# Latent attention: rotary without a permutation matrix, and the softmax of two heads issued in a row

## What is computed

```python
def _rope(x, base):
    ...
    x1, x2 = x[..., :half], x[..., half:]
    return jnp.concatenate([x1 * cos - x2 * sin, x2 * cos + x1 * sin], axis=-1)

def _shared_latent_kv(x, w_down, kv_norm, w_up):
    c = x @ w_down
    lat = _rms_norm(c[..., :KV_LORA], kv_norm)
    k_rope = _rope(c[..., KV_LORA:], ROPE_BASE_B)
    kv = (lat @ w_up).reshape(b, s, H_B, QK_NOPE + V_HEAD)
    return kv[..., :QK_NOPE], k_rope, kv[..., QK_NOPE:]

def block(args):
    sc = (jnp.einsum('bqhd,bkhd->bhqk', qn_i, k_nope)
          + jnp.einsum('bqhr,bkr->bhqk', qr_i, k_rope)).astype(jnp.float32) * scale
    sc = jnp.where(kpos[None, :] <= qpos[:, None], sc, -jnp.inf)
    p = jax.nn.softmax(sc, axis=-1).astype(v.dtype)
    return jnp.einsum('bhqk,bkhd->bqhd', p, v)
```

## Time and profile before

| | before |
|---|---|
| median of 3 runs | 897.47 us (897.4 to 897.61) |
| the profiled execution | 896.96 us |
| its span, first to last instruction | 895.6 us |
| TensorE busy | 887.7 us, 99% of the span |
| VectorE busy | 595.9 us, 67% |
| ScalarE busy | 496.7 us, 55% |
| GpSimd busy | 80.0 us, 9% |
| granted TensorE clock | 1.0 throughout |

### The profile page before, as it was taken

How to read it: one execution, slowest core, us unless ns; L and a number is a source line. 1 busy time by engine, 2 the same in 40 slices (tenths; PEclk the granted TensorE clock), 3 DMA queues, 4 the chain that set the end, 5 groups by cost and what they waited for, 6 DMA issues and landing times.

```text
span 895.6 us, 13337 instructions
## 1 busy us (share of the span) xinstructions
PE 887.7 (99%) x5601; PEld 790.5 (88%) x5601; DVE 595.9 (67%) x801; ACT 496.7 (55%) x629; POOL 80.0 (9%) x58
## 2 busy tenths in 40 slices
PE   9999999999999999999999999999999999999998
PEld 8798887888999999999787899999999888888887
DVE  5876566559866666666568887869767656557441
ACT  6454444435656666666436578797854454545330
POOL 0010101000001111111000000032200011221000
PEclk9999999999999999999999999999999999999999
DMA  9834554642653444455572645423445634545620
GB/s 346 327 131 185 188 194 182 206 154 69 241 184 114 145 147 147 149 188 188 181 257 98 232 147 184 141 95 106 147 172 188 230 127 161 188 166 214 250 98 23
DMA packets 24828, 154.37 MB, mean 172 GB/s; under 512 B 3136, under 2 KB 3520, under 8 KB 9024
## 3 DMA queue, kind: packets, MB, share of 16 engines
q1 hardware_dynamic: 22880, 148.97, 46.1%
q10 hardware_dynamic: 1728, 4.02, 1.6%
q0 software_dynamic: 160, 0.52, 0.1%
HBM read 152.46 MB, written 1.05 MB: 171 GB/s over the span
## 4 chain that ended last, share of the span: by engine, by line
PE 96%; DVE 2%; ACT 1%; DMA 1%; issue 0%; SPq 0%; ACTq 0%
PE ps L338 25%; PE ps L340 25%; PE ps L339 25%; PE ps L389 7%; PE ps L392 3%; PE ps L612 1%; PE ps L637 1%; DMA w_raw<-in_a_w_in 1%; PE ps L617 1%; PE ps L779 1%; PE ps L411 1%; PE ps L807 1%; PE ps L518 1%; PE ps L796 1%; PE ps L627 1%
## 5 line engine op out<-in xcount | busy, mean ns | idle before, releaser
L1420 DVE TENSOR_TENSOR w_lo_ring<-w_raw,w_hi_ring 128x2048 fp32r<-128x2048 f32 x146 | 337.0, 2320 | 183.4 <-ACT w_hi_ring L965 183.2
L965 ACT ACTIVATE w_hi_ring<-w_raw 128x2048 fp32r<-128x2048 f32 x146 | 277.4, 1910 | 109.0 <-PE ps L340 103.7
L338 PE MATMUL ps<-xT_hi,w_hi_ring 128*128 128x256 f32 x520 | 149.4, 287 | 0.5 <-DVE w_lo_ring L1426 0.5
L339 PE MATMUL ps<-xT_lo,w_hi_ring 128*128 128x256 f32 x520 | 147.0, 283 | 0.0
L340 PE MATMUL ps<-xT_hi,w_lo_ring 128*128 128x256 f32 x520 | 147.0, 283 | 0.0
L338 PE MATMUL ps<-w_hi_ring,xT_hi 128*128 128x512 f32 (+1 forms) x272 | 107.4, 395 | 1.4 <-DVE xT_lo L1597 0.6
L340 PE MATMUL ps<-w_hi_ring,xT_lo 128*128 128x512 f32 (+1 forms) x272 | 104.4, 384 | 0.0
L339 PE MATMUL ps<-w_lo_ring,xT_hi 128*128 128x512 f32 (+1 forms) x272 | 104.3, 383 | 0.0
L338 PEld LDWEIGHTS ps<-xT_hi,w_hi_ring 128*128 128x128 f32 x520 | 99.6, 192 | 3.0 <-issue 2.1
L339 PEld LDWEIGHTS ps<-xT_lo,w_hi_ring 128*128 128x128 f32 x520 | 99.6, 192 | 0.6
L340 PEld LDWEIGHTS ps<-xT_hi,w_lo_ring 128*128 128x128 f32 x520 | 99.6, 192 | 0.0
(11 more groups left out here) (328 smaller groups left out, 1647.8 us busy)
## 6 DMA issues: line engine op xcount, KB each, us to landing
w_raw<-in_a_w_in SPq DMA_DIRECT2D x22, 1024.0 KB, 4.9
w_raw<-in_w_ff_in SPq DMA_DIRECT2D x16, 1024.0 KB, 4.9
w_raw<-in_w_ff_out SPq DMA_DIRECT2D x16, 1024.0 KB, 4.8
w_raw<-in_b_w_uq SPq DMA_DIRECT2D x16, 576.0 KB, 4.4
w_raw<-in_a_w_out SPq DMA_DIRECT2D x8, 1024.0 KB, 4.9
w_raw<-in_b_w_gate SPq DMA_DIRECT2D x8, 1024.0 KB, 5.0
w_raw<-in_kv_w_up SPq DMA_DIRECT2D x8, 1024.0 KB, 4.8
w_raw<-in_b_w_out SPq DMA_DIRECT2D x8, 1024.0 KB, 4.8
```

The lines of the kernel that those rows point to most:

```text
L338: k.T.matmul(out, lh, rh, start=start, stop=False, skip_group_check=True)
L339: k.T.matmul(out, lh, rl, start=False, stop=False, skip_group_check=True)
L965: k.A.activation(k.hi[:, u % RING, :], k.raw[u % RING][:, :], ACT.Copy).then_inc(k.s["w_hi"], 1)
L1420: k.V.tensor_tensor(k.lo[:, u % RING, :], k.raw[u % RING][:, :], k.hi[:, u % RING, :].bitcast(F32), ALU.subtract).then_inc(k.s["w_lo"], 1)
```

## The change

The permutation matrix, its table, the copy `b_xr` and the semaphores `b_xr`, `b_rotated`, `b_cos` and `b_sin` go. VectorE multiplies the rotary part by the cosines straight from PSUM, and by the sines in four instructions of 32 partitions each, that write to the partner's 32 partitions (n to n ^ 1); the sign is now in the table of sines. GpSimd only adds. The softmax of a head is in two functions: `dve_masked` and `dve_normal`. VectorE masks both heads in a row, then does `dve_lo(k, u + 1 + AHEAD)`, then normalises both heads; ScalarE exponentiates both heads in a row, ahead of `act_hi(k, u + 1 + AHEAD)`. The output stage has a like order for the last pair. The core of the diff:

```diff
@@ place_latent
-    k.b_rope, k.b_rot, k.b_mask = (k.place(n, s) for n, s in (("ropeB", [P, 2, S]), ("rotB", [P, P]), ("maskB", [P, 3 * P])))
+    k.b_rope, k.b_mask = (k.place(n, s) for n, s in (("ropeB", [P, 2, S]), ("maskB", [P, 3 * P])))
@@ pe_pair
     if pair == 0:
-        T.wait_ge(s["b_xr"], 1)
-        T.matmul(ps[:, 7, 0:S], k.b_rot[:, :], k.b_xr[:, :], start=True, stop=True).then_inc(s["b_rotated"], 1)
         T.wait_ge(s["b_lat"], 1)
...
             if q == 2 and n == 0 and pair:
-                T.wait_ge(s["b_sin"], pair)
+                T.wait_ge(s["b_turned"], pair)
...
-    T.wait_ge(s["b_xr"], pair + 2)
-    T.matmul(ps[:, 2, S:2 * S], k.b_rot[:, :], k.b_xr[:, :], start=True, stop=True).then_inc(s["b_rotated"], 1)
@@ act_pair
     if pair:
         act_exps(k, pair - 1, 0)
+        act_exps(k, pair - 1, 1)
...
     if pair:
         act_pT(k, pair - 1, 0)
-        act_exps(k, pair - 1, 1)
     act_hi(k, u + 3 + AHEAD)
@@ act_attention_output
     act_exps(k, last, 0)
+    act_exps(k, last, 1)
     act_hi(k, U_BOUT + 2 + AHEAD)
     act_pT(k, last, 0)
-    act_exps(k, last, 1)
@@ dve_latents
-    V.tensor_copy(k.b_xr[:, :], ps[:, 6, 0:S]).then_inc(s["b_xr"], 1)
+def dve_rotary(k, x):
+    k.V.tensor_tensor(k.b_xc[:, :], x, k.b_rope[:, 0, :], ALU.mult)
+    for n in range(4):
+        src, dst = slice(32 * n, 32 * n + 32), slice(32 * (n ^ 1), 32 * (n ^ 1) + 32)
+        m = k.V.tensor_tensor(k.b_xs[dst, :], x[src, :], k.b_rope[src, 1, :], ALU.mult)
+    return m
@@ dve_key_rotary
+    own.mark(dve_rotary(k, k.ps[:, 6, 0:S]))
     own.wait()
+    k.V.tensor_tensor(k.b_kr, k.b_xc[:, :], k.b_xs[:, :], ALU.add).then_inc(k.s["b_kr"], 1)
@@ dve_masked: dve_softmax as far as b_pmax; dve_normal: the rest of it
+def dve_normal(k, pair, h):
+    V, s, own, i = k.V, k.s, k.v_own, 2 * pair + h
     V.wait_ge(s["b_pexp"], i + 1)
     own.mark(V.reciprocal(k.b_rsum[:, h, :], k.b_rsum[:, h, :]))
     own.wait()
+    for q, cols in enumerate((slice(0, P), slice(P, 3 * P))):
         m = V.tensor_scalar(k.b_p[:, h, cols], k.b_p[:, h, cols], k.b_rsum[:, h, q:q + 1], None, ALU.mult)
     m.then_inc(s["b_p"], 1)
@@ dve_pair
     if pair:
-        dve_softmax(k, pair - 1, 0)
+        dve_masked(k, pair - 1, 0)
+        dve_masked(k, pair - 1, 1)
...
     dve_lo(k, u + 1 + AHEAD)
+    if pair:
+        dve_normal(k, pair - 1, 0)
+        dve_normal(k, pair - 1, 1)
     dve_lo(k, u + 2 + AHEAD)
     V.wait_ge(s["w_used"], u + 3)
     if pair:
-        V.wait_ge(s["b_cos"], pair)
-    V.tensor_copy(k.b_xr[:, :], ps[:, 2, 0:S]).then_inc(s["b_xr"], 1)
-    if pair:
-        dve_softmax(k, pair - 1, 1)
+        V.wait_ge(s["b_qr"], pair)
+    else:
+        V.wait_ge(s["b_kr"], 1)
+    dve_rotary(k, ps[:, 2, 0:S]).then_inc(s["b_turned"], 1)
     dve_lo(k, u + 3 + AHEAD)
     if pair:
         dve_og(k, pair - 1)
-    V.wait_ge(s["b_rotated"], pair + 2)
-    if pair:
-        V.wait_ge(s["b_qr"], pair)
-    V.tensor_tensor(k.b_xs[:, :], ps[:, 2, S:2 * S], k.b_rope[:, 1, :], ALU.mult).then_inc(s["b_sin"], 1)
@@ dve_attention_output
-    dve_softmax(k, last, 0)
+    dve_masked(k, last, 0)
+    dve_masked(k, last, 1)
+    dve_normal(k, last, 0)
     dve_lo(k, U_BOUT + 2 + AHEAD)
-    dve_softmax(k, last, 1)
+    dve_normal(k, last, 1)
@@ pool_program
-        G.wait_ge(s["b_xr"], pair + 2)
...
-        G.tensor_tensor(k.b_xc[:, :], k.b_xr[:, :], k.b_rope[:, 0, :], ALU.mult).then_inc(s["b_cos"], 1)
-        G.wait_ge(s["b_cos"], pair + 1)
-        G.wait_ge(s["b_sin"], pair + 1)
+        G.wait_ge(s["b_turned"], pair + 1)
         G.tensor_tensor(k.b_qr[:, pair % 2, :], k.b_xc[:, :], k.b_xs[:, :], ALU.add).then_inc(s["b_qr"], 1)
@@ constants
+    sign = np.where(np.arange(P)[:, None] % ROPE < ROPE // 2, 1.0, -1.0)
+    out["k_ropeB"] = np.stack([np.cos(ang), sign * np.sin(ang)], 1).astype(f)
```

More of the change, by code:

```diff
@@ L71 @@
     "o_prod", "ln_t0", "ln_t1",
-    "b_squared", "b_qlat", "b_lat", "b_xr", "b_rotated", "b_kr", "b_gate", "b_scored", "b_pmax", "b_masked", "b_pexp", "b_p",
-    "b_pturned", "b_pT", "b_valued", "b_og", "b_oT_hi", "b_oT_lo", "b_qn", "b_cos", "b_sin", "b_qr", "b_kn", "b_v",
+    "b_squared", "b_qlat", "b_lat", "b_kr", "b_gate", "b_scored", "b_pmax", "b_masked", "b_pexp", "b_p",
+    "b_pturned", "b_pT", "b_valued", "b_og", "b_oT_hi", "b_oT_lo", "b_qn", "b_turned", "b_qr", "b_kn", "b_v",
     "c_sq", "c_total", "c_h0", "c_h1", "c_drain_a", "c_drain_v", "c_kw_hi", "c_kw_lo", "c_sp_in", "c_sp_exp", "sc_even",
@@ L203, in place_latent @@
     k.b_qr, k.b_p, k.b_pT = (k.place(n, [P, 2, c]) for n, c in (("b_qr", S), ("b_p", 3 * P), ("b_pT", 3 * P)))
-    k.b_xr, k.b_xc, k.b_xs = (k.place(n, [P, S]) for n in ("b_xr", "b_xc", "b_xs"))
+    k.b_xc, k.b_xs = (k.place(n, [P, S]) for n in ("b_xc", "b_xs"))
     k.b_og = k.place("b_og", [P, 2, S])
@@ L703, in keys_read @@
     def keys_read():
-        T.wait_ge(s["b_sin"], last + 1)
+        T.wait_ge(s["b_turned"], last + 1)
         T.wait_ge(s["b_kn"], last + 1)
@@ L1018, in act_program @@
     A.wait_ge(s["a_o"], HA)
-    for name, dst in (("k_ropeB", k.b_rope), ("k_rotB", k.b_rot), ("k_maskB", k.b_mask), ("b_q_norm", k.b_qnorm), ("kv_norm", k.b_kvnorm)):
+    for name, dst in (("k_ropeB", k.b_rope), ("k_maskB", k.b_mask), ("b_q_norm", k.b_qnorm), ("kv_norm", k.b_kvnorm)):
         act_dma(k, "tablesB_in", dst[tuple(slice(None) for _ in dst.shape)], d[name])
@@ L1099, in act_latents @@
         if n == 0:
-            A.wait_ge(s["tablesB_in"], 16 * 5)
+            A.wait_ge(s["tablesB_in"], 16 * 4)
         act_turned(k, "qlat", n, ps[:, 1 + n, :], k.b_qlatT[0], k.b_qnorm)
@@ L1628, in dve_latents @@
     V, s, ps, own = k.V, k.s, k.ps, k.v_own
-    V.wait_ge(s["tablesB_in"], 16 * 5)
+    V.wait_ge(s["tablesB_in"], 16 * 4)
     for n in range(4):
@@ L1648, in dve_latents, with dve_masked @@
     m.then_inc(s["b_lat"], 1)
-    V.tensor_copy(k.b_xr[:, :], ps[:, 6, 0:S]).then_inc(s["b_xr"], 1)
-def dve_key_rotary(k):
[L1654 to L1658, removed]
+def dve_rotary(k, x):
[4 more added lines that the diff above has]
+    return m
+def dve_key_rotary(k):
+    own = k.v_own
+    own.mark(dve_rotary(k, k.ps[:, 6, 0:S]))
     own.wait()
-    V.tensor_tensor(k.b_kr, k.b_xc[:, :], k.b_xs[:, :], ALU.add).then_inc(s["b_kr"], 1)
-def dve_softmax(k, pair, h):
-    V, s, ps, own, i = k.V, k.s, k.ps, k.v_own, 2 * pair + h
+    k.V.tensor_tensor(k.b_kr, k.b_xc[:, :], k.b_xs[:, :], ALU.add).then_inc(k.s["b_kr"], 1)
+def dve_masked(k, pair, h):
+    V, s, ps, i = k.V, k.s, k.ps, 2 * pair + h
     qcols = (slice(0, P), slice(P, 3 * P))
@@ L1678, in dve_softmax @@
     own.wait()
-    for q, cols in enumerate(qcols):
+    for q, cols in enumerate((slice(0, P), slice(P, 3 * P))):
         m = V.tensor_scalar(k.b_p[:, h, cols], k.b_p[:, h, cols], k.b_rsum[:, h, q:q + 1], None, ALU.mult)
@@ L2053, in pool_program @@
         G.tensor_tensor(k.a_o[:, 0, :], k.a_o[:, 0, :], k.a_g[:, 0, :], ALU.mult).then_inc(s["a_gated0"], 1)
-    G.wait_ge(s["tablesB_in"], 16 * 5)
     for pair in range(HB // 2):
```

## The result

The changed kernel takes 900.67 us (median of 6 runs, 900.21 to 901.23), the kernel before on the same chip 897.38 us (896.76 to 897.61). The ratio is 1.0039, with a 95% interval of 1.0027 to 1.0051: slower by 3.3 us. The forecast was 901.9 us, 4.4 us slower.

The account below looks back on a forecast made before the run. TensorE was taken to bound the kernel: -4.10 us of permutation matmuls, -0.6 in the output stage and +9.1 of waits give +4.4, so 901.9 us from the median 897.47. The range was 899.2 to 905.0 us.

Parts of the forecast that it names:

- What bounds, and what the change saves on TensorE: TensorE, busy 887.7 of 895.6 us, sets the end; permutation matmuls L686 and L651 taken away save 4.10 us.
- The wait: In pairs 1 to 7 TensorE waits at L627 for head 0's probabilities, 1.3 us each, 9.1 us in all.
- rival (d): Masking of head 1 ends after ScalarE finishes head 0; longer wait, up to 907.8 us; margin 0.15 us; 7%.
- The last pair: Output stage: head 1, masked earlier, is normalised before TensorE needs it; gain 0.6 us.
- The rotary costs nothing: VectorE's rotary, 0.33 + 4 x 0.41 = 2.0 us, ends before work needed later; nothing charged.
- rival (c): Rotary quarters of 1.2 us or more make TensorE wait before the scores; 914 us at the upper bound; 3%.
- (a): The wait at the turn stays hidden and only the savings remain: 892.8 us; 6%.
- (b): The wait is half as long, 0.4 to 0.9 us a pair; time stays near 897.5 us; 6%.

Follow-up runs that it names:

- e4: The changed kernel with ScalarE's exponentials of head 1 moved behind act_hi(u + 1 + AHEAD): 894.33 us, the kernel before 896.92 us.
- e1: The changed kernel with VectorE normalising head 0 ahead of the split dve_lo(u + 1 + AHEAD): 892.14 us, the kernel before 896.92 us.
- e2: The changed kernel with the old softmax order, in the output stage too, and the new rotary kept: 899.74 us, the kernel before 896.92 us.
- e9: e2 with the rotary moved behind the masking and normalisation of head 1: 892.75 us, the kernel before 897.06 us.
- e5: The changed kernel with both normalisations behind dve_lo(u + 2 + AHEAD), so two splits stand ahead: 926.98 us, the kernel before 896.64 us.

## Why the prediction was right, and where it was not

**What bounds, and what the change saves on TensorE.** Right. Eight L686 at 0.43 us; and in pair 0 and 1 the sums hold: the first scores load weights at 264.90 in the changed kernel and 266.19 before, 1.29 us earlier, of which 0.43 is L686, 0.66 the keys' matmul, and 0.16 lies ahead of the change; 0.04 is not accounted for.

**The wait.** Right in mechanism and nearly in size: 1.23 us, not 1.3. The chain itself, from the start of masking to the turn's weight load, was forecast at 321.94 - 314.33 = 7.61 us and is 322.19 - 314.61 = 7.58. Each link was where it was put: exponentials of head 1 0.90 us behind those of head 0 (315.48, 316.38), the split 1.93 us behind the high part, the reciprocal 2.20 behind the split. Masking head 1 ended in the shadow of head 0's exponentials (316.11 + 0.17 = 316.28 against 316.38), as rival (d) would not have it; the margin was 0.10 us, not 0.15. e4 and e1 show that this chain is the cause, by taking one link and then all of it away. Seven times 1.3 instead of 1.23 accounts for 0.5 of the 1.1 us by which the forecast was too high; the output stage, below, gives 0.14, and the 0.16 ahead of the change is no effect of it.

**The last pair.** Right in kind, a little small: scores of the last pair start 4.24 us later than before (430.31 against 426.07 in the chain) and the end 3.5 us later, so the output stage gave back 0.74 us, not 0.6. With the 0.16 us at the start this leaves, by rows, 7 x 1.23 - 3.44 - 0.66 - 0.74 - 0.16 = +3.6 us against +3.5 in the spans.

**The rotary costs nothing.** Right for the changed kernel and wrong as a statement on the rotary. The quarters are 0.42 us each and 0.43 apart, near the 0.41 taken, and rival (c) didn't come. The whole takes 2.2 us and not 2.0, because the first quarter too starts only behind the end of the product ahead of it (324.91 + 0.42 = 325.33, against a start at 325.35), 0.44 us behind its start, where the sum took 0.33. But the prediction looked only at what stands behind the rotary in the new order, and priced the new order in the pairs as pure loss. e2 shows what it missed: in the old order the masking of head 1 stands behind the rotary, and there it costs 2.8 + 4.1 = 6.9 us. So the two halves of the change are not two terms of a sum. Alone, the rotary is 2.8 us slower and the order 8.4 us slower; together they are 3.3, not 11.2. Masking both heads in a row takes head 1 out of the rotary's way, which is what the rotary needs; the fault lies in one thing only, that the normalisations were put behind a split. e9 shows that moving the rotary does as well as moving the masking.

**The rivals.** (a) and (b), 6% each, did not come. (a)'s 892.8 us is what e1 reaches with one line moved, 892.14.

**A longer wait.** The prediction priced a wait by its length alone. e5 shows the range in which that holds: at 1.23 us it does, at 3.2 to 3.4 us TensorE's clock fell after every wait and 1.5 us a pair came on top.

## To carry to other kernels

When an instruction is moved within a queue, list what it now stands behind, and follow that back through the other engines: here a normalisation of 0.75 us was put behind a split that waits for a high part that waits for another exponential, 5 us of chain for a slack of 3.7 us. Do the same for each half of a change alone and for both together; here either half lost, one hid part of the other's loss, and one line turned the sum into a gain. Work without a near consumer (the splits, the rotary) belongs behind the work that TensorE will ask for next.

## What the runs showed of the hardware that I had not expected

In e5 TensorE's granted clock did not fall during the wait, in which TensorE stood nearly idle from 328.8 to 332.3, but 1.1 us after it had resumed: it was 1.00 from 332.3 to 333.4 and 0.50 from 333.4 to 336.8, and the products in that stretch started 0.21 us apart instead of 0.12. The waits of 1.23 us in the changed kernel had nothing of the kind.

On VectorE, products of 32 partitions that read PSUM and write to another group of 32 partitions took 0.41 to 0.43 us for 256 columns, as those of 128 partitions do, and 0.27 to 0.30 us for 128 columns.

In pair 0 of the changed kernel GpSimd's add started together with a split of VectorE and took 2.85 us, where the same add takes 0.74 us in a later pair. Its row in the timeline, and VectorE's beside it:

```profile
259.12 2.85 POOL L2068 TENSOR_TENSOR b_qr<-b_xc,b_xs 128x256 f32<-128x256 f32 x1 [96.06 <-DVE b_xs L1653]
```

```profile
259.07 2.29 DVE L1416 TENSOR_TENSOR w_lo_ring<-w_raw,w_hi_ring 128x2048 fp32r<-128x2048 f32 x1
```

It ended at 261.97, ahead of the scores at 264.90, so it cost nothing here. No run here tried what held it back.
